# Copy of the turned keys ahead of the row decays of the chunk behind, in ScalarE's order of a mixer step

## What is computed

```python
# gated delta rule: decays within a chunk, and a triangular system
decay = where(causal, exp(gc_i - gc_j), 0)
m     = where(strict, (k_beta @ k.T) * decay, 0)          # solved for u, w
a     = (q @ k.T) * decay
v_new = u - w @ state
o     = (q * exp(gc)) @ state + a @ v_new
state = state * exp(gc_last) + (k * exp(gc_last - gc)).T @ v_new

# HGRN2: per-channel decay
o      = (q * exp(bcum)) @ hstate + scores @ v
hstate = exp(last) * hstate + (k * exp(last - bcum)).T @ v
```

## Time and profile before

| | us |
|---|---|
| median of 3 runs | 1392.7 |
| lowest and highest | 1391.06, 1399.81 |
| the profiled execution, its own time | 1391.73 |
| its span, first to last instruction | 1389.9 |

### The profile page before, as it was taken

One profiled execution on the slowest core, in us unless ns is written; L12 is line 12 of the kernel. 1 busy time (PEld: TensorE's weight loads), 2 busy tenths in 40 slices (PEclk: granted clock), 3 DMA queues, 4 the chain that ended last, 5 costly groups with the idle time before them and its releaser, 6 DMA issues.

```text
span 1389.9 us, 24260 instructions
## 1 busy us (share of the span) xinstructions
PE 1334.3 (96%) x9101; PEld 1110.0 (80%) x9101; DVE 783.0 (56%) x1171; ACT 591.8 (43%) x1403; POOL 674.5 (49%) x583
## 2 busy tenths in 40 slices
PE   5999999999999888888999999999999999999997
PEld 4777887978888777777888788888888888788886
DVE  5014635557354588785147955555555556665657
ACT  6234535444343556552133433333333334344445
POOL 3233324143253577660210876766666777654442
PEclk9999999999999999898999999999999999999999
DMA  5131312423226333514210245444554545886663
GB/s 183 33 104 50 104 61 79 126 65 120 64 78 158 115 101 91 172 56 156 61 31 1 83 130 162 148 161 157 174 174 144 174 144 205 300 276 192 189 195 121
DMA packets 160371, 178.60 MB, mean 128 GB/s; under 512 B 9520, under 2 KB 110464, under 8 KB 160256
## 3 DMA queue, kind: packets, MB, share of 16 engines
q1 hardware_dynamic: 160112, 176.53, 40.1%
q10 hardware_dynamic: 144, 0.52, 0.1%
HBM read 124.32 MB, written 52.71 MB: 127 GB/s over the span
## 4 chain that ended last, share of the span: by engine, by line
PE 85%; DVE 4%; issue 4%; ACT 3%; POOL 2%; DMA 1%; SPq 0%; DVEq 0%; ACTq 0%; POOLq 0%
PE banks L2416 9%; PE banks L2417 9%; PE banks L2418 9%; PE banks L353 6%; PE banks L355 6%; PE banks L354 6%; PE banks L2427 4%; PE banks L2429 4%; PE banks L2428 4%; PE banks L692 2%; PE banks L693 2%; PE banks L694 2%; PE banks L2108 2%; PE banks L2110 2%; PE banks L2109 2%
## 5 line engine op out<-in xcount | busy, mean ns | idle before, releaser
L2574 POOL TENSOR_TENSOR w_l<-area,w_h 128x512 fp32r<-128x512 f32 x119 | 175.5, 1480 | 180.0 <-ACT w_h L2469 135.0
L2574 POOL TENSOR_TENSOR w_l<-w_raw,w_h 128x512 fp32r<-128x512 f32 x100 | 140.5, 1406 | 99.7 <-ACT w_h L2524 50.3
L353 PE MATMUL banks<-act_h,w_h 128*128 128x512 f32 x352 | 141.4, 402 | 0.0
L355 PE MATMUL banks<-act_h,w_l 128*128 128x512 f32 x352 | 137.5, 391 | 0.0
L354 PE MATMUL banks<-act_l,w_h 128*128 128x512 f32 x352 | 137.3, 390 | 0.0
L341 POOL TENSOR_TENSOR w_l<-w_raw,w_h 128x1024 fp32r<-128x1024 f32 x24 | 59.4, 2478 | 142.5 <-ACT w_h L334 125.3
L2416 PE MATMUL banks<-act_h,w_h 128*128 128x512 f32 x320 | 124.5, 389 | 0.0
L2417 PE MATMUL banks<-act_l,w_h 128*128 128x512 f32 x320 | 124.5, 389 | 0.0
L2418 PE MATMUL banks<-act_h,w_l 128*128 128x512 f32 x320 | 124.5, 389 | 0.0
L2427 PE MATMUL banks<-w_h,act_h 128*128 128x512 f32 x308 | 120.1, 390 | 0.3 <-DVE act_l L2726 0.3
L2428 PE MATMUL banks<-w_l,act_h 128*128 128x512 f32 x308 | 119.9, 389 | 0.0
(11 more groups left out here) (316 smaller groups left out, 3353.3 us busy)
## 6 DMA issues: line engine op xcount, KB each, us to landing
w_raw<-in_w_in SPq DMA_DIRECT2D x22, 512.0 KB, 4.1
w_raw<-in_w_gate SPq DMA_DIRECT2D x22, 512.0 KB, 4.6
area<-in_w_up SPq DMA_DIRECT2D x22, 512.0 KB, 4.8
ff_wide<-in_w_down SPq DMA_DIRECT2D x22, 512.0 KB, 4.4
down_sums<-ff_wide SPq DMA_DIRECT2D x11, 1024.0 KB, 4.1
area<-in_x SPq DMA_DIRECT2D x8, 1024.0 KB, 8.0
projected_tm<-area SPq DMA_DIRECT2D x32, 256.0 KB, 2.4
hidden_sums<-area SPq DMA_DIRECT2D x6, 1024.0 KB, 4.2
```

Of the source, the lines that this page charges most:

```text
L353: e.matmul(dst, w_h[:, b, k], act_h[:, k, cols], start=(k == 0), stop=False)
L355: mm = e.matmul(dst, w_l[:, b, k], act_h[:, k, cols], start=False, stop=(k == KT - 1))
L2574: e.tensor_tensor(slot(w_l, u), raw_use(u) if u < NU_FF else wd_raw(u - NU_FF), slot(w_h, u).bitcast(F32), ALU.subtract).then_inc(sems["fl ...
```

## The change

In ACT's `step(t)` of the mixer two calls change places. The copy of the turned keys of chunk t now stands ahead of the row decays of chunk t + 2. Nothing else is changed: the same instructions with the same waits and buffers, on all engines.

```diff
@@ -1673,10 +1673,10 @@
                 if live(t):
                     squares(t)
                     lengths(t)
+                if live(t, NT - 1):
+                    keys_turned(t)
                 if live(v):
                     decays(v)
-                if live(t, NT - 1):
-                    keys_turned(t)
                 if live(u):
                     inverse(u, 5)
                     whole_inverse(u)
```

## The result

| | median, us | lowest to highest | runs |
|---|---|---|---|
| before | 1391.2 | 1390.5 to 1399.8 | 8 |
| changed | 1383.4 | 1378.3 to 1386.5 | 8 |

The ratio is 0.993, with a 95% interval of 0.991 to 0.995: 7.8 us faster, 0.6%. The forecast was 1381.3, its range 1378.5 to 1387.5. The profiled execution of the changed kernel took 1385.8 us, so it is one of the slower ones, and that will matter.

A forecast was written before the change was run, and what follows sets the result against it. No single engine bounds a mixer step; hand-overs with idle time do, plus a clock falling behind TensorE's thin stretch. 6.3 + 4/6 x (12.5 - 6.3) = 10.4 us off 1391.7 gives 1381.3, range 1378.5 to 1387.5.

The forecast's parts named there:

- upper sum: Mixer steps 0 to 5: clock stays at 2.4 GHz over `key_key`, DVE's idle time is gained, 12.5 us after deductions.
- the mix: Over the six changed steps: clock holds in four and falls in two, 6.3 + 4/6 x (12.5 - 6.3) = 10.4 us.
- The copy: ACT at t = 1: reaches the copy 0.46 us before the keys; TensorE's 1.01 us wait for it is gone.
- What is late next: TensorE at t = 1: `key_key` then waits for DVE's L1794 and starts 0.9 us earlier; 0.1 of the 1.01 is lost.
- The clock in the changed steps: TensorE over `key_key`, steps 0 to 5: the granted clock holds in four of six steps and falls in two.
- POOL idled 1.47 us before 511.14, so I charge nothing more: POOL's low half follows ACT's later split of output weights; its idle time was taken to cover this, no further charge.
- DVE is then the bound: Step t = 1 at full clock: `key_query` ends by 508.8, DVE is ready at 508.6; the step gains 1.8 us.
- lower sum: Steps 0 to 5, clock falling as now: all behind `key_key` comes 0.9 us earlier a step, 6.3 us in all.

The follow-up runs named there:

- the changed kernel again: The changed kernel, unaltered, run again for its spread and a second profile: 1382.4 us, ratio 0.9925.
- the entry filled: The changed kernel with seven identity matmuls more, once, in mixer step 0 ahead of `update(1, 1)`: 1383.4 us, ratio 0.994.
- step 6 filled: The changed kernel with eleven identity matmuls more in mixer step 6, ahead of `update(7, 5)`: 1377.7 us, ratio 0.992.
- `unit` moved: The changed kernel, no fillers, with POOL's `unit(v)` moved from the front of a step to the end of the one before: 1380.0 us, ratio 0.9925.
- the wait put back: The changed kernel with `gated_state` on TensorE also waiting for the absolute values of the decays, steps 0 to 5: 1388.2 us, ratio 0.999.

## Why the prediction was right, and where it was not

The time, 1383.4, is within the range, and the sign and size are right to a quarter (7.8 for 10.4). The mechanism of the upper sum is shown; that the whole came this near is in part luck (the mix, below). By the steps:

- **The copy.** Right. ACT waits 0.35 us for the keys (0.46 forecast), TensorE's wait for it is 0, the decays are done at 509.42 and are read at 511.56.
- **What is late next.** Right: `key_key` now waits for L1794, 0.39 us at t = 1 and 1.6 us in all, and starts 1.0 us behind L1239's end (0.9 forecast).
- **The clock in the changed steps.** Right in kind and a little too low: over `key_key` it held in five of six steps of this profile, not four. In the four other profiles of the new order without fillers in steps 1 to 5 (the changed kernel again, the entry filled, step 6 filled, `unit` moved) it held in five, four, five and five.
- **The upper sum, 12.5.** Right for steps 1 to 5: they gave 9.7, for which the rows of DVE's idle time had 13.8 - 3.2 = 10.6. Of the missing 0.9 us, 0.2 is left of the old waits, 0.6 is the new wait for `key_state`, a hand-over that the sum did not follow, and 0.1 is longer work of DVE. "POOL idled 1.47 us before 511.14, so I charge nothing more" was wrong as a reason, for POOL does get late and meets the scans (2.3 us longer), but L1769 gives 1.7 of that back, so that in the sum it comes to little. For t = 0 the sum had 2.3 us, and the first profile has the changed kernel 4.1 late there. That is the low clock at the entry: in the second profile, where the clock was back at 468 as in the kernel before, L1749 of t = 0 starts at 483.3, 3.4 us earlier than before. In the working, "DVE is then the bound" did not follow from its own rows either: they had TensorE's end at 508.8 and DVE ready at 508.6, and the gated output then took less than the 1.85 us allowed for it (511.28 - 509.99 = 1.29).
- **The lower sum, 6.3. Wrong.** It took the wait as worth its length. With the gap's place kept and the clock held up by fillers the gain was all there (ratio 0.992); with the gap put back and the order kept it was nil (0.999); at a full clock the order is worth 0.3 to 1 us in all. At a low clock two steps of the new order took 24.2 and 24.7, no less than before. My reading of it: a wait of TensorE that ends 1 us earlier in a loop where DVE is busy 20 of 24 us gains little, for DVE has its own queue to finish before it needs the products; only the slow `key_key` and `gated_out` behind it had made TensorE the later of the two. The two steps with the gap and a full clock, 22.5 and 22.9, bear that out.
- **The mix, 6.3 + 4/6 x 6.2.** It came out near the result because errors offset. It is a third of the lower sum and two thirds of the upper, 2.1 + 8.3; the 2.1 should have been next to nothing, the clock held oftener than in four of six, and I had nothing for the entry. There the changed kernel is 4.1 us later in the profile, at L1749 of step 0, with the clock low to 488.4. The kernel before can lose time to a low clock too, though no profile shows where: its slowest runs beside the experiments, 1396.7 to 1399.1, have a mean clock of 0.975 to 0.978, where the common 1390 goes with 0.985.
- **The spread.** Not foreseen. Six of the first eight runs of the kernel before lie within 1 us, but the other two are 1392.7 and 1399.8, and beside the experiments its 17 runs spread over 10 and 11 us, the last 11 over 2. The changed one spreads over 8. In the profile of before the clock fell in every changed step; in the five profiles of the new order without fillers in steps 1 to 5 it was low over `key_key` in one or two of them, not always the same. That the thin stretch is now caught in some runs only would fit this, but is not shown for the times of the single runs.

What stays open: why the clock comes back at once at the entry in some executions, after 20 us in others, and does not fall there at all in some (step 6 filled, the wait put back). Up to there the kernel before and the changed one do the same work within 0.1 us, and the changed kernel shows both courses in its own two profiles, so the order of the two calls doesn't decide it. In the kernel with the entry filled the fall came later, and in the others it moves without a filler too, so not even that the filler moved it is shown. The order's worth at a low clock rests on two steps.

## What to carry to other kernels

Here a gap of about 1 us on TensorE cost 1.5 us or next to nothing, and the gap's length doesn't tell which: look at the granted clock of the work right behind it, and compare the same matmuls where the clock is full. Before reordering another engine's queue to close such a gap, fill it with matmuls that nobody reads: that takes four lines, shows what the clock alone is worth, and here was as good as the change. And when a chain is pulled forward past an engine off the path, look where that engine's work now falls, for it may meet instructions that it had missed before.

## What the runs showed of the hardware

Beside a busy POOL, a scan of 128 x 128 on DVE took up to 0.94 us instead of 0.40, and three multiplications of 128 x 128 took 2.83 us instead of 0.68 beside a subtraction on POOL of 2.45; it was the reordering, not any added work, that made them meet. The granted clock fell behind a stretch of TensorE work that was thin but had no wait longer than 1.01 us in it (busy 1.86 of 3.40 us), and with four matmuls of 128 x 128 in that wait, in each of six steps, the profiled execution stayed at 2.4 GHz for 146 us of mixer. The Trainium skill, page TensorE: Matmul & The Clock Gate, describes in its section on a second HAM failure mode a bf16 kernel whose clock falls for frequent small gaps between groups of matmuls; these float32 runs agree with it. Its section on HAM oscillation is about long pauses for a DMA, and this stretch has none. The same program on the same data took 1378.3 us at a mean granted clock of 0.993 or 1386.5 at 0.982: a single profile of such a kernel shows one case of several.
